# Retention values in 512-column matmuls over half-contraction slabs, with the retention steps moved later

## The reference, cut to what matters

```python
q_r, k_r = h @ w_in[...]            # 8 heads x 64
v_r = h @ w_in[...]                 # 8 heads x 128: the retention values, 1024 columns
g_r = h @ w_in[...]                 # 1024 columns: the gate of the retention branch
# retention, as this kernel computes it for each head over all 512 tokens:
s = (q_r @ k_r.T) * decay           # causal, decay[i - j] of the head
o = s @ (v_r - mean(v_r))           # v centred, so that o has mean 0
on = o * rsqrt(mean(o * o) + 1e-5) * gain
r_out = silu(g_r) * on
# after it: mixed = gate_a * (a_out @ w_a) + gate_r * (r_out @ w_r); x = x + mixed @ w_out
```

## Time and profile before

| | us |
|---|---|
| median of 3 runs | 1724.09 (1724.0 to 1724.63) |
| the profiled execution | 1723.94 |
| its span, first to last instruction | 1722.0 |
| TensorE (PE) busy in it | 1686.9 (98%) |
| VectorE (DVE) busy | 1027.0 (60%) |
| ScalarE (ACT) busy | 645.1 (37%) |

### The profile page before, as it was taken

How to read it: one execution, slowest core, us unless ns; L and a number is a source line. 1 busy time by engine, 2 the same in 40 slices (tenths; PEclk the granted TensorE clock), 3 DMA queues, 4 the chain that set the end, 5 groups by cost and what they waited for, 6 DMA issues and landing times.

```text
span 1722.0 us, 22517 instructions
## 1 busy us (share of the span) xinstructions
PE 1686.9 (98%) x8985; PEld 1338.6 (78%) x8985; DVE 1027.0 (60%) x1667; ACT 645.1 (37%) x1017; POOL 60.6 (4%) x84
## 2 busy tenths in 40 slices
PE   7999999999999999999999999999999999999899
PEld 6888888787866678768888888888888866677687
DVE  5665444456887756347444457643554587878674
ACT  4222222241257742333222233312222567556830
POOL 0000000000012210000000000000000000002200
PEclk9999999999999999999999999999999999999999
DMA  6655433246300015313333233324332333402322
GB/s 204 207 163 176 133 98 90 74 125 195 94 1 2 2 53 146 96 49 81 104 94 97 89 105 98 91 84 121 89 96 81 101 104 98 132 10 62 92 80 73
DMA packets 235372, 167.61 MB, mean 97 GB/s; under 512 B 10437, under 2 KB 221629, under 8 KB 235141
## 3 DMA queue, kind: packets, MB, share of 16 engines
q1 hardware_dynamic: 232948, 161.98, 32.4%
q10 hardware_dynamic: 2320, 4.20, 0.7%
HBM read 156.31 MB, written 6.30 MB: 94 GB/s over the span
## 4 chain that ended last, share of the span: by engine, by line
PE 87%; DVE 8%; ACT 2%; issue 1%; SPq 1%; DMA 1%; POOL 0%; DVEq 0%; ACTq 0%
PE bank L1070 24%; PE bank L1072 24%; PE bank L1071 24%; PE turned L1319 3%; PE bank L1307 2%; PE bank L1345 2%; PE bank L1492 1%; PE bank L1409 1%; DVE w_lo L1722 1%; DVE Pm L2420 1%; DVE bank L2113 1%; PE bank L1618 1%; PE turned L1398 1%; ACT Pm L1016 1%; PE turned L1128 1%
## 5 line engine op out<-in xcount | busy, mean ns | idle before, releaser
L1070 PE MATMUL bank<-h_hi,w_hi 128*128 128x512 f32 x1200 | 472.6, 394 | 3.0 <-DVE h_lo L1777 1.5
L1071 PE MATMUL bank<-h_lo,w_hi 128*128 128x512 f32 x1200 | 467.3, 389 | 0.0
L1072 PE MATMUL bank<-h_hi,w_lo 128*128 128x512 f32 x1200 | 467.2, 389 | 0.0
L649 ACT ACTIVATE w_hi<-w_raw 128x2048 fp32r<-128x2048 f32 (+3 forms) x134 | 236.8, 1767 | 490.6 <-PE bank L1072 490.0
L1722 DVE TENSOR_TENSOR w_lo<-w_raw,w_hi 128x2048 fp32r<-128x2048 f32 (+3 forms) x133 | 280.0, 2106 | 55.3 <-ACT w_hi L649 52.6
L1070 PEld LDWEIGHTS bank<-h_hi,w_hi 128*128 128x128 f32 x1200 | 225.2, 188 | 60.2 <-issue 11.6
L1072 PEld LDWEIGHTS bank<-h_hi,w_lo 128*128 128x128 f32 x1200 | 225.3, 188 | 47.3
L1071 PEld LDWEIGHTS bank<-h_lo,w_hi 128*128 128x128 f32 x1200 | 225.3, 188 | 46.6 <-issue 0.7
L1070 PE MATMUL bank<-u_hi,w_hi 128*128 128x512 f32 x352 | 137.1, 389 | 0.0
L1071 PE MATMUL bank<-u_lo,w_hi 128*128 128x512 f32 x352 | 137.0, 389 | 0.0
L1072 PE MATMUL bank<-u_hi,w_lo 128*128 128x512 f32 x352 | 136.9, 389 | 0.0
(11 more groups left out here) (425 smaller groups left out, 2359.9 us busy)
## 6 DMA issues: line engine op xcount, KB each, us to landing
w_raw<-in_w_in SPq DMA_DIRECT2D x28, 1024.0 KB, 5.5
w_raw<-in_ffn_w_gate SPq DMA_DIRECT2D x44, 512.0 KB, 4.0
w_raw<-in_ffn_w_up SPq DMA_DIRECT2D x44, 512.0 KB, 5.3
w_raw<-in_ffn_w_down SPq DMA_DIRECT2D x32, 704.0 KB, 4.6
ada_w<-in_ada_w SPq DMA_DIRECT2D x16, 768.0 KB, 6.6
w_raw<-in_w_in SPq DMA_DIRECT2D x19, 512.0 KB, 4.2
w_raw<-in_w_out SPq DMA_DIRECT2D x8, 1024.0 KB, 5.0
w_raw<-in_w_branch_nsa SPq DMA_DIRECT2D x8, 512.0 KB, 5.5
```

What stands on the lines that cost most here:

```text
L649: act.activation(w_hi[s % 2][:, 0:n], w_raw[s % 2][:, 0:n], ACT.Copy).then_inc(s_hi, 1)
L1070: pe.matmul(o, l[0], r[0], start=first, stop=False)
L1071: pe.matmul(o, l[0], r[1], start=False, stop=False)
L1072: return pe.matmul(o, l[1], r[0], start=False, stop=last)
```

## The change

The values are projected in two halves of 512 columns. Each half has two slabs: contraction slices 0 to 3, then 4 to 7, all 512 columns wide. In the first slab of a half the four token tiles are opened, one in each bank, 12 matmuls of 512 columns each; in the second they are finished with 12 more each. So 8 accumulators are closed, all in the second slab of a half. The retention steps begin with the second half: step i behind each of its 8 groups of 12 matmuls, steps 8 to 15 in gate tiles 0 and 1, and step 16, `r_sums` and the two `r_spread` one gate tile later each. ACT and DVE follow: four heads an evacuation, one `centre` over 512 columns, moved `decays`, `weights_low`, `pair_moments`, `spread_scale`.

```diff
-        rsum = at("rsum", [P, NT, 2], F32, ARENA + 98 * KB)
+        rsum = at("rsum", [P, NT, 4], F32, ARENA + 98 * KB)
-        stage("rv", [cols_slab(wi, (c, c + 256)) for c in range(W_RV, W_RG, 256)], 16)
+        stage("rv", [cols_slab(wi[:, k:k + 4, :], (c, c + 512), kt=4) for c in (W_RV, W_RV + 512) for k in (0, 4)], 8)
 # ACT: value_rows, pair_moments, rg
-                for e in range(2):
-                    ins = act.activation(rv[:, t, s * 256 + e * P:s * 256 + e * P + P], bank[a % 4][:, e * P:e * P + P], ACT.Copy,
+                for e in range(4):
+                    ins = act.activation(rv[:, t, s * 512 + e * P:s * 512 + e * P + P], bank[a % 4][:, e * P:e * P + P], ACT.Copy,
...
-                if s >= 2 and t == 0:
-                    pair_moments(s - 2)
-            each_slab("rv", value_rows, 4)
+                if i == 4:
+                    pair_moments(0)
+            each_slab("rv", value_rows, 2)
             def rg(i, a):
-                if i < 2:
-                    pair_moments(2 + i)
+                if i < 3:
+                    pair_moments(1 + i)
...
-                if i == 1:
+                if i == 2:
                     act.wait_ge(sem("r_sums"), 1)
 # PE
-            for s in range(4):
-                wh, wl = use_slab()
-                for t in range(NT):
-                    token_tile(wh, wl, KD, (h_hi, h_lo), t, 256)
-                    if s:
-                        r_step(4 * s - 4 + t)
+            for half in range(2):
+                a0 = acc_at[0]
+                for part in range(2):
+                    wh, wl = use_slab()
+                    for t in range(NT):
+                        if part == 0:
+                            pe.wait_ge(acc_free, a0 + t - 3)
+                        tokens = slice(t * P, (t + 1) * P)
+                        for k in range(4):
+                            ins = mm3(bank[(a0 + t) % 4][:, :], (h_hi[:, 4 * part + k, tokens], h_lo[:, 4 * part + k, tokens]),
+                                      (wh[:, k, :], wl[:, k, :]), part + k == 0, part * k == 3)
+                        if part:
+                            close_acc(ins)
+                        if half:
+                            r_step(4 * part + t)
                 def beside_gate(k):
-                    if m == 0 and k % 2 == 0:
-                        r_step(12 + k // 2)
-                    if (m, k) == (1, 0):
+                    if m < 2 and k % 2 == 0:
+                        r_step(8 + 4 * m + k // 2)
+                    if (m, k) == (2, 0):
                         r_step(16)
-                    if (m, k) == (1, 5):
+                    if (m, k) == (2, 5):
                         r_sums()
-                    if (m, k) in ((2, 6), (3, 6)):
-                        r_spread(m - 2)
+                    if (m, k) in ((3, 6), (4, 6)):
+                        r_spread(m - 3)
 # DVE (centre is now one instruction over 4 heads)
-            for i in range(16):
+            rope_r(7)
+            weights_low()
+            for i in range(4):
                 centre(i)
-                if i == 0:
-                    rope_r(7)
-                if i >= 4:
-                    decays(i - 4)
-                if i % 4 == 3:
+            for i in range(6):
+                decays(i)
+                if i in (1, 5):
                     weights_low()
+            for i in range(4, 8):
+                centre(i)
+                if i < 6:
+                    decays(i + 2)
+            weights_low()
...
             for m in range(KD):
-                if m == 0:
-                    for i in range(12, 16):
+                if m < 2:
+                    for i in range(8 + 4 * m, 12 + 4 * m):
                         decays(i)
-                if m == 1:
+                if m == 2:
                     dve.wait_ge(sem("r_std"), 1)
                     done(dve.reciprocal(rinv[:, :], rstd[:, :]), "r_inv")
                 scale_tile(rsil[m % 4][:, :])
                 if m % 2:
                     weights_low()
-                if m == 2:
+                if m == 3:
                     spread_scale(0)
                 if m in (3, 4, 5):
                     gated(2 * m - 6)
                     gated(2 * m - 5)
-                if m == 3:
+                if m == 4:
                     spread_scale(1)
```

More of the change, by code:

```diff
@@ L1403, in r_values @@
                 pe.wait_ge(sem("r_m"), 2 * i + 2)
-                pe.wait_ge(sem("rv_ready"), i + 1)
+                pe.wait_ge(sem("rv_ready"), p // 2 * NT + kb + 1)
                 if kb == 0 and p:
@@ L2212, in centre @@
                 acc_at[0] += 1
-                v = rv[:, t, s * 256:(s + 1) * 256].rearrange("p (e n) -> p e n", e=2)
+                v = rv[:, t, s * 512:(s + 1) * 512].rearrange("p (e n) -> p e n", e=4)
                 freed()
-                tick(dve.scalar_tensor_tensor(v, rsum[:, t, :].unsqueeze(2).to_broadcast([P, 2, P]), -1.0 / P, v, ALU.mult, ALU.add), "rv_ready")
+                tick(dve.scalar_tensor_tensor(v, rsum[:, t, :].unsqueeze(2).to_broadcast([P, 4, P]), -1.0 / P, v, ALU.mult, ALU.add), "rv_ready")
             def decays(i):
```

## The result

The changed kernel takes 1730.61 us (median of 8 runs, 1728.49 to 1732.04), the kernel before beside it 1724.32 (8 runs): ratio 1.0036, 95% interval 1.0027 to 1.0045, which is 4.7 to 7.8 us more. Slower, as forecast; 1729.9 was predicted, in a range of 1726.0 to 1731.3. The profiled execution took 1728.49 us, 4.55 more than the one before, its span 1726.7 against 1722.0.

What follows compares the result with a forecast made beforehand. PE's matmul stream, 87% of the chain, was taken as the bound. -2.52 + 0.5 + 0.77 + 0.35 + 3.39 = +2.49 us, plus 3.44 for two clock falls, on 1723.94 gave 1729.9, range 1726.0 to 1731.3.

Steps and rivals of the forecast that it cites:

- The matmuls: Value projection: 192 matmuls of 512 columns replace 384 of 256 columns, 2.52 us less.
- The steps moved at no cost: Four retention steps changing sides between value and gate tiles: same cost in either place, bounds 0 and 0.1 us each.
- Wait 1: PE before the third value slab, waiting for its split weights in the second half: 0.5 us.
- Wait 2: PE before step 9, waiting for decays(8) behind DVE's low part: 2.8 us, 0.77 more than the waits before.
- Wait 3: PE before `r_sums`, with `pair_moments(3)` on ACT now behind the split of the third gate slab: 0.35 us.
- Wait 4: PE before r_spread(1), with `spread_scale(0)` on DVE now behind the last gate slab's low part: 3.39 us.
- The clock: Granted clock falls behind the waits before step 9 and r_spread(1): 1.72 us each, 3.44 together; two falls, chance 0.40.
- one fall: Rival: only one of the waits before step 9 and r_spread(1) lowers the clock, 1728.2 us; chance 0.33.
- both longer than the one that did: Waits of 2.8 us before step 9 and 3.4 before r_spread(1) exceed the 2.38 us idle that preceded a fall.
- Faster: Rival: the new waits don't bind, at most down to 1719.4 us; chance 0.03.
- It doesn't do what it says: Rival: a 512-column matmul costs as much as two short ones, 2.52 us lost, 1732.4; counted within worse, 0.07.
- No fall: Rival: the clock stays full behind the new waits, 1726.4 us, +0.14%; chance 0.17.

Runs made afterwards that it cites:

- decays(8) first: The changed kernel with decays(8) on DVE ahead of the low part of the second gate slab: 1726.48 us, ratio 1.0018 to the kernel before.
- five additions: The kernel without the four waits, with five useless 128x512 additions on DVE ahead of `spread_scale(0)`: 1726.60 us, ratio 1.0015 to the kernel before.
- the late r_spread: The kernel before with only both `r_spread` on PE and both `spread_scale` on DVE one gate tile later: 1729.54 us against 1723.42, ratio 1.0037.
- the control: The changed kernel run once more, unaltered: 1728.91 us against 1723.83 for the kernel before, ratio 1.0031.
- kernel without waits: The changed kernel with four waits removed by reordering DVE and ACT: 1719.29 us, ratio 0.9976 to the kernel before; again, 1720.78 us, ratio 0.9985.
- `spread_scale` first: The changed kernel with `spread_scale(0)` on DVE ahead of `weights_low` in gate tile 3: 1725.33 us, ratio 1.0005 to the kernel before.
- the one with short matmuls: The kernel without the four waits, each 512-column value matmul issued as two of 256 columns: 1723.56 us against 1720.78 without this edit.

## Why the prediction was right

The sum was built from terms that can be held against the traces one by one.

*The matmuls.* Predicted -2.52; putting the short ones back cost 2.25. The distances in the first half of the values are what the rows said: 0.2267 (670.06 to 691.60, 95 distances). Beside the steps the gain is smaller, and the prediction took the undisturbed distances for all: ten distances behind step 1 take 2.29 us, 0.229 each (702.25 to 704.54), where 22 short ones of before took 2.63, 0.1195 each (691.79 to 694.42).

*The steps moved at no cost.* Right within what the traces show: step 5, behind a group of the values, takes from 718.11 to 721.33, 3.22 us, and step 13 of the same width, now in gate tile 1, from 749.11 to 752.38, 3.27.

*Wait 1*, predicted 0.5, measured 0.51. *Wait 2*, predicted 2.8, measured 2.42. The prediction took 2.0 us of wait for the kernel before. In that lie 0.28 us that `r_values` and the scores behind it need without any wait (in the changed kernel 729.24 to 730.30, 1.06 where 0.78 stand before a projection matmul). The true waits before are 0.43 and 1.30, together 1.73, and the term, predicted +0.77, comes to +0.69. *Wait 3*, predicted 0.35, measured 0.22. *Wait 4*, predicted 3.39, measured 3.48; it was called the one that decides, and without it the kernel is level with the one before (1.0005).

*The clock.* Here the prediction was right in kind and not in count. It took the nearest row, 2.38 us of idle with a fall, as if any longer wait had to bring one. It said two falls; the profiled execution has one, and its 1728.49 us is the rival "one fall" (1728.2) to 0.3 us. The step that failed is "both longer than the one that did". The prediction held 2.8 us, counted from start to start, against 2.38 us of idle. In idle time, by its own figures, wait 2 is 0.36 + 1.22 + 0.77 = 2.35 us, and 2.34 was measured: no longer than the example. Of three executions with that wait one has a fall. Behind 3.4 us of idle all five profiles have one (the changed kernel and its repeat, decays(8) first, five additions, the late r_spread). Two of the signs that it named came otherwise. The low level began as PE resumed and not 1.5 us later (the stretch from 782 to 783 reads 0.75, the two behind it 0.50). And the stage is 4.69 us longer and not 5 to 6.

So the closeness of 1729.9 to the median of 1730.61 is partly luck: the two profiles of the changed kernel show +4.69 and +4.63 us, with one fall each, and the control's median is +5.1. The upper group of times lies some 3 us above the lower one. A fall behind step 9 (1.54) and one at 518 us, outside the stage (1.53, last section), would together give 3.1; that is an estimate, and no profile shows such an execution. The granted clock of a whole span, 0.996 or 0.997 in either group, doesn't tell them apart. What lengthens the upper group stays open.

*The sum in the trace.* With the measured terms: -2.25 - 1.73 + 0.51 + 2.42 + 0.22 + 3.48 + 1.58 = +4.23 against 4.69 in the stage. The kernel without waits gives -2.25 - 1.73 = -3.98 against -3.66. So 0.3 to 0.5 us in both are not placed, and the cost of the moved steps, taken as nothing, may be in them.

*The rivals.* "Faster" named its own condition, all waits together under 1.1 us. The kernel without waits meets it and is faster, by order on DVE and ACT alone. "It doesn't do what it says" is out by the pair of kernels that differ in shape only. "No fall" is out for these executions: each of the five profiles with a wait of 3.4 us has one.

## What to carry to other kernels

When work is moved by one tile in a program written out by hand, ask of every engine what stands ahead of it in the new place: here an even tile became an odd one, and the 2.3 us weight conversion with its own wait came in front of an instruction that had 0.28 us to spare. A matmul stream that is 98% busy repays a saving of 2 us only if each hand-over's slack is known; four reorderings without any new work turned +5 us into -3 to -4. And a wait of the matmul engine can cost its length and a stretch at half clock behind it: here that came behind every wait of 3.4 us, behind some of 2.0 to 2.7, and at one place behind 1.4.

## What was not expected of the hardware

The fall of the clock is not fixed by the length of the wait. The second block has a wait of 2.4 us of idle in all 13 profiles, with the same code around it. In 8 of them the mean granted clock from 1526 to 1545 us is 0.91, in 5 it is 1.00. The row of the changed kernel, which is one of the 8, reads the same in the kernel with `spread_scale` first, which is one of the 5:

```profile
PE bank L1612 <- ACT dv L994: 2.4, 1, 2.4
```

What such a fall costs depends on what PE has to do behind it. In this place the next projection matmul comes 92.2 to 92.5 us after the wait in the five profiles without a fall and 93.0 to 93.4 in the eight with one, so it costs 0.8 to 1.1 us and not the 1.72 that the prediction took from its row.

Nor does it need a long wait. In the first block, at about 518 us, PE waits 1.37 us with some short waits around it, the same in all 13 profiles. In 6 of them the clock falls there (both profiles of the kernel without waits, the one with short matmuls, both single edits to the changed kernel, five additions), and from this wait to the first value matmul it takes 153.3 to 153.4 us instead of 151.8, 1.5 more. The changed kernel and the kernel before have no fall there in their profiles. First the kernel without waits, then the kernel before:

```profile
518.62 0.66 PE L1339 MATMUL turned<-cst,sc 128*128 128x128 f32 x4 [1.37 <-DVE sc L2126]
520.00:522.00 2.00, 2.00 (x17) 1.45 (x14) 0.15 (x1) 0.82 (x4) 0.00 (x0) 0.50 0.03 8
...
518.58 0.66 PE L1330 MATMUL turned<-cst,sc 128*128 128x128 f32 x4 [1.37 <-DVE sc L2108]
520.00:522.00 2.00, 2.00 (x28) 1.71 (x28) 1.26 (x10) 1.47 (x6) 0.54 (x1) 1.00 0.03 8
```

These falls come and go with the code unchanged, and are a likely part of why the runs of one kernel scatter over 3 us; the timed runs have no profiles that would show it. It is also why two executions are best compared stage by stage. The Trainium skill ("TensorE: Matmul & The Clock Gate", "What's actually happening") names two states of the clock, half and full, and nothing between them; the rows agree, 0.50 in the whole microseconds of the low stretch and 0.43 us between 512-column matmuls against 0.23.
